# A hybrid decoder step: no meeting ahead of attention, the scan's 16-row chunk taken last, its norm moved behind the scan, and pairs of tiles in the tail

## The reference

```python
x = x + 0.5 * swiglu(x)                         # feed-forward 1
q,k,v,qi,ki,wi,z,xbc,dt,ga,gs = split(rmsnorm(x) @ w_in)
q, k = rmsnorm(q), rmsnorm(k)
# attention: index scores, the best 256 keys of each query, softmax over them
s = where(kpos <= qpos, (wi * relu(qi @ ki)).sum(heads), -inf); idx = top_k(s, 256)
A = softmax(q @ k[idx] / 8) @ v[idx]
# state space: causal convolution of 4 taps, SiLU, then the scan by chunks
xs, B, C = split(silu(conv(xbc)))
acs = cumsum(dt * Aneg)                         # inside a chunk
y = (C B^T * exp(acs_i - acs_j) * dt_j, j <= i) @ xs + (C @ h) * exp(acs)
h = h * exp(acs_last) + B^T @ (xs * exp(acs_last - acs) * dt)
y = (y + d_skip * xs) * silu(z)
S = y * rsqrt(mean(y*y over each of 4 groups of 512) + eps) * g_norm
x = x + (sigmoid(ga) * (A @ w_attn_out) + sigmoid(gs) * (S @ w_ssd_out)) @ w_o
x = x + 0.5 * swiglu(x)                         # feed-forward 2
```

## Time and profile before

| what | us |
|---|---|
| median of 3 runs | 3760.57 (3759.28 to 3767.15) |
| the profiled execution, its own time | 3765.35 |
| its span | 3763.6 |
| TensorE matmul busy | 3558.8 (95%), 22152 matmuls |
| VectorE, GpSimd, ScalarE busy | 2034.0, 1537.7, 809.1 |
| mean granted TensorE clock | 0.954 of full speed |

### The profile page before, as it was taken

How to read it: one execution, slowest core, us unless ns; L and a number is a source line. 1 busy time by engine, 2 the same in 40 slices (tenths; PEclk the granted TensorE clock), 3 DMA queues, 4 the chain that set the end, 5 groups by cost and what they waited for, 6 DMA issues and landing times.

```text
span 3763.6 us, 56718 instructions
## 1 busy us (share of the span) xinstructions
PE 3558.8 (95%) x22152; PEld 3365.0 (89%) x22152; DVE 2034.0 (54%) x3182; ACT 809.1 (21%) x1628; POOL 1537.7 (41%) x679
## 2 busy tenths in 40 slices
PE   8999999998999999997789989898999899999998
PEld 7999999988968999997688846668999799999998
DVE  5343333365758999976456545883164533333334
ACT  2000000012231111333555425661210200000000
POOL 2534534423313444443376006774344245344351
PEclk9999999999989999998699977999999999999999
DMA  2111211102202222232432126753342012111111
GB/s 86 57 39 39 59 36 45 55 23 80 62 27 79 90 92 88 90 95 68 48 113 79 46 63 168 186 135 119 102 149 61 28 46 61 34 47 53 33 56 56
DMA packets 399842, 272.29 MB, mean 72 GB/s; under 512 B 61842, under 2 KB 375522, under 8 KB 399720
## 3 DMA queue, kind: packets, MB, share of 16 engines
q1 hardware_dynamic: 379896, 225.75, 22.1%
q10 hardware_dynamic: 19824, 44.95, 3.2%
HBM read 211.05 MB, written 59.81 MB: 72 GB/s over the span
## 4 chain that ended last, share of the span: by engine, by line
PE 85%; DVE 6%; ACT 4%; issue 2%; DMA 1%; SPq 1%; POOL 1%; another core or an unknown queue 0%; DVEq 0%; ACTq 0%; POOLq 0%
PE setA L353 10%; PE setA L354 10%; PE setA L355 10%; PE setB L353 9%; PE setB L354 9%; PE setB L355 9%; PE bankC L353 2%; PE bankC L355 2%; PE bankC L354 2%; PE bankD L355 2%; PE bankD L353 2%; PE bankD L354 2%; PE bankC L1418 2%; PE setA L1436 2%; PE setB L1436 2%
## 5 line engine op out<-in xcount | busy, mean ns | idle before, releaser
L345 POOL TENSOR_TENSOR whi<-wraw,ones 128x1024 fp32r<-128x1024 f32 x192 | 464.3, 2418 | 1686.8 <-PE setA L355 1077.2
L353 PE MATMUL setA<-hhi,whi 128*128 128x352 f32 (+1 forms) x2304 | 758.6, 329 | 41.5 <-issue 15.0
L354 PE MATMUL setA<-hlo,whi 128*128 128x352 f32 (+1 forms) x2304 | 751.2, 326 | 0.0
L355 PE MATMUL setA<-hhi,wlo 128*128 128x352 f32 (+1 forms) x2304 | 750.0, 326 | 0.0
L353 PE MATMUL setB<-hhi,whi 128*128 128x352 f32 (+1 forms) x2304 | 746.7, 324 | 0.0
L354 PE MATMUL setB<-hlo,whi 128*128 128x352 f32 (+1 forms) x2304 | 742.8, 322 | 0.0
L355 PE MATMUL setB<-hhi,wlo 128*128 128x352 f32 (+1 forms) x2304 | 741.5, 322 | 0.0
L353 PEld LDWEIGHTS setA<-hhi,whi 128*128 128x128 f32 x2304 | 440.8, 191 | 50.4 <-issue 24.1
L348 POOL TENSOR_TENSOR wlo<-wraw,whi 128x1024 fp32r<-128x1024 f32 x192 | 473.3, 2465 | 15.0
L354 PEld LDWEIGHTS setA<-hlo,whi 128*128 128x128 f32 x2304 | 440.9, 191 | 2.0
L355 PEld LDWEIGHTS setA<-hhi,wlo 128*128 128x128 f32 x2304 | 440.5, 191 | 0.0
(11 more groups left out here) (417 smaller groups left out, 5768.0 us busy)
## 6 DMA issues: line engine op xcount, KB each, us to landing
wraw<-in_w_in SPq DMA_DIRECT2D x64, 512.0 KB, 3.8
wraw<-in_w_ffn_gate SPq DMA_DIRECT2D x44, 512.0 KB, 3.8
wraw<-in_w_ffn_up SPq DMA_DIRECT2D x44, 512.0 KB, 3.8
wraw<-in_w_ffn_down SPq DMA_DIRECT2D x44, 512.0 KB, 3.5
abc<-acsD SPq DMA_DIRECT2D x8, 2048.0 KB, 9.8
xcD<-cv ACTq DMA_DIRECT2D x24, 520.0 KB, 2.7
xc<-xcD SPq DMA_DIRECT2D x8, 1536.0 KB, 14.5
zD<-spill ACTq DMA_DIRECT2D x16, 524.0 KB, 2.7
```

Of the source, the lines that this page charges most:

```text
L345: pool.tensor_tensor(dst_cols(slot, hi), dst_cols(slot), ones[:, :].unsqueeze(1).to_broadcast([P, KD, P]), ALU.mult).then_inc(w_hi, 1)
L353: pe.matmul(out, w1, r1, start=start, stop=False)
L354: pe.matmul(out, w1, r2, start=False, stop=False)
L355: return pe.matmul(out, w2, r1, start=False, stop=stop)
```

## The change

- `gemm_pair` waits for the split of its second tile only where it starts that tile, and parts 1 to 3 of the tail take their first two tiles with it.
- The chunk of 16 rows is the last of the nine (`tok0`, `width`, the store of the token rows); the loop over chunks has two passes and the other chunks are written out.
- Meeting 0 is gone. In its place each engine waits for what it needs: SP for the last projection and the stored convolutions, DVE for the convolution's buffers, TensorE for the index scores and its banks. The other meeting has number 0.
- `query_high` of block 0 and four `key_high` stand in the convolution loop, behind ScalarE's last `xraw` copies. Keys are split in two pieces of columns, 0:128 and 128:1040 (`KEYS`); the second piece comes in units 2 to 9 (ScalarE) and 4 to 11 (DVE).
- TensorE's transposes of the sample's convolution state stand before the first scores.
- ScalarE issues exp(u+1) ahead of the copy of unit u.
- The sample's norm in the sample stage is gone; `rss` is copied into `sums`, columns L:T.
- In the scan the gate writes in place into `zc`, the norm per chunk is gone and the sums of squares of all tokens stay in `sums`. SP's order for chunk c is: wait for `y2_ready`, load `abc`, `xc` and `tc` of c+2, store `zc` of c, wait for the squares and that store, load `zc` of c+2. The front waits for three loads (48), the gate for `z_loaded`.
- Behind the scan ScalarE takes two square roots of 2x1048 columns, DVE two reciprocals, and `dve_rows` scales `sraw` by `gssd` and the reciprocal in 24 instructions for each of parts 1 and 2. `act_high` then writes a third of `hhi` in one instruction. The second load of `sraw` starts at m = 1 instead of 3.
- `sample_state` on GpSimd takes a chain object for its order instead of two semaphores.

```diff
-            pe.wait_ge(w_split, n + 2)
+            pe.wait_ge(w_split, n + 1)
...
+                    if j and c == 0:
+                        pe.wait_ge(w_split, n + 2)
...
-                return (0, META) if c == 0 else (META + (c - 1) * P, P)
+                return (c * P, P) if c < NCH - 1 else (SEQ, META)
...
+                if b == CONVD // P - 1:
+                    act.wait_ge(qk_ready, NU)
+                    query_high(act, 0)
+                    for i in range(4):
+                        key_high(act, i, 0)
                 out(b - 1)
...
+            exps(0)
+            for u, (t, pos) in enumerate(AU):
+                if u + 1 < len(AU):
+                    exps(u + 1)
...
-                if t == 0 and pos < 4:
-                    key_high(4 + pos)
+                if t == 0 and pos < 2:
+                    for i in range(2):
+                        key_high(act, 4 + 2 * pos + i, 0)
+                elif t == 0 and pos < 2 + 2 * NKV:
+                    key_high(act, pos - 2, 1)
...
+            def turn(c, slot, used, nxt):
+                sp.wait_ge(y2_ready, c * SG + SG)
+                if nxt is not None:
+                    load_in(nxt, slot)
+                    load_tok(nxt, slot)
+                store_rows(c, slot)
+                if nxt is not None:
+                    sp.wait_ge(ysq_ready, c * SG + SG)
+                    sp.wait_ge(slot_out[slot], used * 16 + (SSD_OUT1 + 16))
+                    load_z(nxt, slot)
...
-                    pe.wait_ge(chunk_loaded[slot], used * 64 + 64)
+                    pe.wait_ge(chunk_loaded[slot], used * 48 + 48)
...
-            def norm(c, slot):
-                v.wait_ge(root_done, c + 1)
-                v.reciprocal(ss4[:, slot, :, 0:w], ss4[:, slot, :, 0:w]).then_inc(rstd_ready, 1)
-                for g in range(SG):
-                    v.tensor_tensor(y2[:, slot, bs, 0:w], y2[:, slot, bs, 0:w],
-                                    ss4[:, slot, g:g + 1, 0:w].to_broadcast([P, GB, w]), ALU.mult).then_inc(norm_ready, 1)
...
+            for h, dst in enumerate((sums[:, 0:2, :], rs23[:, :, :])):
+                act.activation(dst, sums[:, 2 * h:2 * h + 2, :], ACT.Sqrt, bias=eps[:, 0:1], scale=1.0 / GW)
...
-                for m in range(2):
-                    gemm_tile(pe, n + m, q, m, ready=(part_ready, 3 * s) if m == 0 else None)
+                gemm_pair(pe, n, q, (part_ready, 3 * s))
...
+        def dve_rows(v, s):
+            r = sums if s == 1 else rs23
+            v.wait_ge(rstd_ready, s)
+            v.wait_ge(sraw_loaded, 16 * s)
+            for c, (o, w) in enumerate(CH):
+                for k in range(KD):
+                    b = KD * (s - 1) + k
+                    ins = v.scalar_tensor_tensor(sraw[:, k, o:o + w], sraw[:, k, o:o + w], gssd[:, b:b + 1],
+                                                 r[:, k // GB, o:o + w], ALU.mult, ALU.mult)
+                ins.then_inc(rows_ready, 1)
```

More of the change, by code:

```diff
@@ L1450, in outputs @@
                     mm.then_inc(ot_done, 1)
-            scores(0)
-            scores(1)
+            pe.wait_ge(idx_relu, len(IDX_UNITS))
+            for j in range(2):
+                pe.wait_ge(gemm_evac[j], 3 * ORD_AO)
             pe.wait_ge(st_loaded, 32)
@@ L1457, in pe_attn @@
             mm.then_inc(tail_done, 1)
+            scores(0)
+            scores(1)
             pe.wait_ge(tail_evac, 2)
@@ L1588, in outputs, with exps @@
                             .then_inc(ot_evac, 1)
-            for u, (t, pos) in enumerate(AU):
-                w = WID[t]
+            def exps(u):
+                w = WID[AU[u][0]]
                 act.wait_ge(s_masked, u + 1)
@@ L1720, in dve_attn @@
                         dn += 1
+                        if dn == 1:
+                            for j in range(2):
+                                v.wait_ge(slot_out[j], SSD_OUT0)
                         v.wait_ge(pt_done[1], dn)
@@ L1729, in dve_attn @@
                     result(u - 1)
-                if t == 0 and 1 <= pos < 5:
-                    key_low(3 + pos)
+                if t == 0 and 1 <= pos < 3:
+                    for i in range(2):
+                        key_low(2 + 2 * pos + i, 0)
+                elif t == 0 and 4 <= pos < 4 + 2 * NKV:
+                    key_low(pos - 4, 1)
                 if t == 1:
@@ L1846, in over_chunks @@
             step(1, 1, 0, 2)
-            with eng.Fori(0, (NCH - 3) // 2) as i:
+            with eng.Fori(0, (NCH - 5) // 2) as i:
                 step(i * 2 + 2, 0, i + 1, i * 2 + 3)
                 step(i * 2 + 3, 1, i + 1, i * 2 + 4)
-            step(NCH - 1, 0, NCH // 2, None)
+            for c in range(NCH - 3, NCH):
+                step(c, c % 2, c // 2, c + 1 if c < NCH - 1 else None)
         def wait_u(eng, s, c, g, back):
@@ L1908, in sp_ssd @@
             load_ao(sp, 1)
-            sp.wait_ge(y2_ready, 4)
-            load(2, 0)
-            step(0, 0, 0, 1)
-            with sp.Fori(0, (NCH - 3) // 2) as i:
-                sp.wait_ge(y2_ready, i * 8 + 8)
-                load(i * 2 + 3, 1)
-                step(i * 2 + 1, 1, 0, None)
-                sp.wait_ge(y2_ready, i * 8 + 12)
-                load(i * 2 + 4, 0)
-                step(i * 2 + 2, 0, 0, None)
-            step(NCH - 2, 1, 0, None)
+            turn(0, 0, 0, 2)
+            with sp.Fori(0, (NCH - 5) // 2) as i:
+                turn(i * 2 + 1, 1, i, i * 2 + 3)
+                turn(i * 2 + 2, 0, i + 1, i * 2 + 4)
+            for c in range(NCH - 4, NCH):
+                turn(c, c % 2, c // 2, c + 2 if c < NCH - 2 else None)
             load_ao(sp, 2)
-            step(NCH - 1, 0, 0, None)
         part_hi = sem("part_hi")
         part_ready = sem("part_ready")
+        rs23 = at("rs23", [P, 2, T], F32, AR + 2 * XB)
         fin_st = at("fin_st", [P, NXB // 4, 4, P], F32, mboff + DI * 4 + NXB * P * 4)
@@ L2076, in part_high @@
                 act.activation(hhi[:, :, o:o + w], qT[:, :, o:o + w], ACT.Identity).then_inc(part_hi, 1)
+            act.activation(sums[:, :, L:T], rss[:, :, :], ACT.Identity).then_inc(rss_in, 1)
             exps(0, 0, 0, 0)
-            over_chunks(act, step)
+            for c in range(NCH):
+                step(c, c % 2, c // 2, c + 1 if c < NCH - 1 else None)
             part_high(2, 4 * NCH)
@@ L2188, in step @@
                         weights(n[0], n[1], ns)
-                    if g == 2 and not (isinstance(c, int) and c == 0):
-                        norm(c - 1, 1 - slot)
             v.wait_ge(hT_zero, 1)
@@ L2204, in dve_ssd @@
                     state(NCH - 1, SG - 1)
[L2205 to L2209 removed]
+            v.wait_ge(slot_out[1], Y_OUT0[1])
+            for h, t_ in enumerate((sums[:, 0:2, :], rs23[:, :, :])):
+                for m in (2 * h, 2 * h + 1):
+                    v.wait_ge(fin_done, m + 1)
+                    v.tensor_copy(fin_st[:, m, :, :], CD[m % 2][:, :].rearrange("p (b n) -> p b n", n=P))\
+                        .then_inc(fin_evac, 1)
+                v.wait_ge(root_done, h + 1)
+                v.reciprocal(t_, t_).then_inc(rstd_ready, 1)
         mixed = at("mixed", [P, KD, T], F32, R1)
@@ L2378, in dve_tail @@
         def dve_tail(v, ch):
-            dve_part_scaled(v, 1, sraw)
-            dve_part_scaled(v, 2, sraw)
+            for s in (1, 2):
+                dve_rows(v, s)
+                for c in range(3):
+                    dve_low_part(v, s, sraw, c)
             def mix(m, c):
```

219 lines of the change are left out of this document (97 added, 122 removed).

## The result

The changed kernel takes 3710.07 us (median of 4 runs, 3709.17 to 3713.6), against 3762.67 for the kernel before in the same comparison: ratio 0.9861, interval 0.9844 to 0.9878. It is faster, by 52.6 us where 91 were forecast, and lies above the range. The profiled execution took 3709.17 us (span 3707.4).

The account below looks back on a forecast made before the run. TensorE, busy 95% of the span, was taken as the bound, so only its idle or half-clock time counts. Six terms summed to 91.3 us: 3669 from the median 3760.57, taken as 3670; own range 3657 to 3686, ends 3646 and 3706.

Parts of the forecast that it names:

- term 6: Tail: paired tiles shorten the seams, row scalings cost nothing; gain 14 us, bounds 5 to 18.
- term 1: Meeting ahead of attention: removed, with query and key splits earlier; gain 14.5 us, bounds 8 to 19.
- Term 4: Scan: load waits and VectorE's norm go, TensorE becomes the bound; gain 26 us, bounds 8 to 31.
- Term 2: Attention loop: exp ahead of the evacuation cuts TensorE's waits; gain 24 us, bounds 5 to 46.
- rival C: Last attention block and part of the sample stage run at full clock: 14 us more, 3656; chance 0.12.
- Term 3: Seam to the scan: sample norm, a table load and chunk 0's z wait go; gain 3.4 us, bounds 1 to 4.
- Term 5: Scan to first projection: reciprocal and scalings ahead of the last gate go; gain 9.4 us, bounds 3 to 12.
- A: Scan: the DMA chain still ends last, 8 chunks lose 20 us: 3690; chance 0.15.
- B: Attention gains little, 7 us instead of 24: 3687; chance 0.12.
- D: Scan: half clock does not end, slower than before, 3850 with seven such chunks; chance 0.05.
- E: The removed meeting and norms were hidden anyway: 30 us of gain in all, 3730; chance 0.06.
- The sign that I had named: Profile after the change: under 2.5 us of idle time at each of the tail's four seams.

Follow-up runs that it names:

- meta_first: The changed kernel with the 16-row chunk in front again, all else as changed: 3704.15 us, ratio 0.9836.
- best_last: The changed kernel with 128 rows (zeros added) in the last chunk, single tiles at the tail's seams, second sraw load behind the fourth tile: 3662.22 us, ratio 0.9725.
- both: The changed kernel with the 16-row chunk in front and single tiles at the seams of the tail: 3682.59 us, ratio 0.9773.
- tail_tiles: The changed kernel with the first two tiles of tail parts 1 to 3 as single tiles again: 3691.95 us, ratio 0.9802.
- wide_end: The changed kernel with the last chunk's matmuls on all 128 columns instead of 16, still 16 rows: 3726.03 us, ratio 0.99.

## Why the prediction was wrong, point by point

The step that failed is in term 6: "a pair waits about 0.7 for the second tile's split, and the tile after it 1.28". The waits were 5.81 and 6.27 us at part 1, 5.82 and 1.46 at part 2. The price was taken from a pair with VectorE idle. At both seams VectorE runs its low parts, and at part 1 also the 24 row scalings, which I had booked at nothing as "DVE is idle 134 us there". They hold GpSimd's splits (9.5 us for 4.8, and 7.38 for 2.4), and a pair wants the split 4 us after its own start; in term 1 I had charged VectorE for that same collision and in term 6 forgot the other side. With single tiles and the rows later the seams of parts 1 and 2 have no wait, and the tail takes 402.1 to 403.3 us instead of 415.5: the 14 us of term 6 were there without the pairs. At part 3 the pair's own waits came as priced (1.32 us behind the pair, 1.20 at the last pair for a forecast of 1.1), but its first third came 8.4 us after part 2, against 1.8 before; VectorE's low part of it took 5.25 us beside a split.

Term 4 failed in "it halves the same amount of time; ... 3". The steady part came out as forecast (seven chunks in 184.5 us, 26.4 each, no wait for loads from chunk 3 on). But the short chunk at the end brings its own fall of the clock, 42.4 us for its four groups (2438.1 to 2480.5); and it multiplies with the state, which the first chunk skips. The order cost 13.3 us (meta_first), not 3. The rows behind the wrong step were right, have clock 0.50 for the 16-row chunk, but I took that as left over from the idle time ahead and did not ask whether the chunk would lower the clock by itself.

What held: term 1 (12.8 for 14.5). The collision was there and larger than the 2 us booked: the last taps took 7.92 us beside the query's low parts (5.83), against 3.98.

```profile
1769.03 7.92 DVE L1124 SCALAR_TENSOR_TENSOR cv<-xraw,cw,cv 128x1040 f32<-128x1040 f32 x3 [4.21 <-ACT cv L998]
1770.02 5.83 POOL L1320 TENSOR_TENSOR qs<-qT,qs 64x1024 fp32r<-64x1024 f32 x2 [19.96 <-ACT qs L1229]
```

Term 2 gave 33.2 for 24: block 0 nothing, as forecast, block 1 2.2 for 6, block 2 5.8 for 5, the middle 18.5 for 10, the last block 7.1 for 3 (its clock 0.85 for 0.60). The ScalarE sum of block 0 adds up to 27.2 and not 27.5, which changes nothing. Of rival C only the last block's part came (4.1 us of its 14). These are figures of one profile each, and loops with the same code lie up to 18 us apart, so the excess over 24 may be luck. Term 3 gave 0.6 for 3.4. The load of chunk 0 was again waited for (2.99 us, now tc; before 4.35, zc), and the sample stage was 0.8 longer; what in it was, stays open. Term 5's own part held: 4.5 us from the last gate to the projection. In term 4, VectorE's relief was a cause: with its work back the chunks take 31.0 us. That the front no longer waits for z is one in the changed order (37.3 us with the wait back); how much it was worth in the order of before isn't shown. Rivals A, B, D and E did not come. No case of mine had the tail lose. The sign that I had named did show it: idle time under 2.5 us at each seam, where the changed kernel has 12.1, 7.3 and 9.7 at parts 1 to 3.

The two failed steps close the balance: best_last has them mended (the chunk stays last, with 128 rows) and takes 3662, 47.9 below the changed kernel, by 19.7 us in the scan and 27.3 in the tail (47.0).

What stays open: why the attention loop differs between executions. In the trace of the kernel called both (358.1 us) GpSimd waited 17.4 us for the broadcast load of the first sample state, in that of tail_tiles (342.0 us) 8.2 us, and the next query's low parts stand behind it; that this is the cause was not tried.

## What to carry to other kernels

A pair of tiles moves the second tile's weight split a whole tile earlier and frees the buffers of both at once: price it by when each split may start and what VectorE does beside GpSimd at that time, not by a pair elsewhere. The short chunk cost 13 us less in front, where the clock was low anyway, than at the end, where it had been high, and padding its rows to 128 with zeros was cheaper than leaving them out (scan 245.7 for 261.7 us). Where two things make a stage late, as the scan's loads and VectorE here, removing one alone can show nothing: with VectorE's work back, the split loads left the chunks at 31.0 us (before 30.5).

## What the runs showed of the hardware

With 128 columns, a group took 10.0 us at full clock where the products with es have 16 rows (wide_end) and 6.6 us where all have 128: fewer rows made TensorE slower. With 16 columns and 128 rows it took 5.2 us. In each form of the last chunk the granted clock fell to half although the records show TensorE busy without a gap. With 16 rows, at 16 and at 128 columns, it stayed there 48 and 58 us; with 128 rows 17 us, and 24 where 112 of them are zero. Beside GpSimd, VectorE's two-input instructions and GpSimd's own both stretch: 3.98 to 7.92 us (three convolution taps) and 2.4 to 7.38 us (one high part of the weight split).
